# Rows of every second expert built on TensorE instead of gathered, and each expert's down product moved behind the next expert's gate and up

## The chip, the cores and the metric

One core of one Trainium2 chip runs the whole program. The metric is the device time of one execution in microseconds (us), of which less is better.

## What is computed

Two transformer layers over 512 prompt tokens and 32 sample tokens (8 streams of 4), model width 1024, all in fp32. Layer 0 mixes with a latent attention (a cache of 4096 rows for each sample stream), layer 1 with a window attention. After each of them stands a mixture of 32 experts, and that is the part that the change touches:

```python
def hier_moe(x, w_group, b_group, w_expert, b_expert, w_gate, w_up, w_down):
    ...
    g_p, g_idx = lax.top_k(g_prob, 1)
    e_top, e_idx = lax.top_k(e_sel, TOP_K_IN_GROUP)          # 2 experts for a token
    gate = g_p * jax.nn.softmax(e_top, axis=-1)
    ...
    def run_block(args):
        xb, e = args
        hid = jax.nn.silu(xb @ w_gate[e]) * (xb @ w_up[e])   # 1024 -> 512
        return hid @ w_down[e]                               # 512 -> 1024
```

544 tokens with two experts each make 1088 rows over 32 experts, 34 on average. The weights of one expert are three matrices of 2 MiB, 6.29 MB together, and every expert's weights are read from HBM once a layer: 201 MB a layer.

## The kernel before

The kernel is written engine by engine, with semaphores between the engines; no scheduler moves anything, so the order of the lines is the order on each engine. `x`, the residual rows, lies in SBUF as five tiles of 128 tokens (`TILES` = 5). The expert part is `experts(L)`, which exists once for each engine. A block takes at most `BLK` = 64 rows of one expert; more rows would go through a second loop (`more_...`).

- **Which rows.** VectorE (DVE) makes a matrix of marks for expert q, `mark(q)`: 128 x 5 x 64, a one where a token of this tile is the expert's row r. TensorE (PE) multiplies the marks with token numbers (`numbers(q)`: 5 small matmuls), and DVE turns the product into an index list.
- **Fetching rows.** Normalized rows have been stored to HBM (`moe_rows_in`). GpSimd (POOL) gathers the rows of expert q by an indirect DMA into `xe[q % 2]`, `LOOK` = 3 experts ahead, and PE turns them by 8 transposes (`fetched_T`); ScalarE (ACT) copies them to `xeT` (`rows_T`). Only expert 0's rows are made otherwise: its marks, multiplied with each token's reciprocal root (`direct`), are PE's stationary operand, the raw rows `x` its moving one (10 matmuls of 512 columns), and DVE applies the gain while it copies the turned rows to `xeT[0]`.
- **The expert.** PE: gate and up for k = 0..7 (16 matmuls of 64 x 512 outputs), then the transposes of the next expert's rows, `numbers(e + 3)`, 4 transposes of `hid`, and down (8 matmuls). ACT computes the silu, DVE the product `hid`, and the copy `hidT` of the turned `hid`. ACT and DVE copy half each of the result out (`y0_ready`, `y1_ready`), and POOL scatters it to HBM (`moe_rows_back`).
- **Weights.** SyncE (SP) issues the loads in the order gate, up, down of expert 3, 4, and so on, into `SLOTS` = 3 buffers. Its wait rule, which the change leaves alone, is:

```python
def follow(e, s):
    sp.wait_ge(sig["gu_mm"], happened("gu_mm", NE * L + e - 2))   # gate and up of expert e - 3 done
    gate_up(e, s)
    sp.wait_ge(sig["d_mm"], happened("d_mm", NE * L + e - 2))     # down of expert e - 3 done
    down(e, s)
```

Each fp32 matmul stands as two MATMUL records in the trace: the 24 of an expert's down and the next one's gate and up are "x48". PE's matmuls are recorded at L1941 and its transposes at L1946, both helpers; L996 is the silu, L1600 the product `hid`, L1605 the copy `hidT`, L1611 the copy of the result, L681 the gather, L691 the scatter, L500 the gate and up loads, L505 the down loads.

Of the kernel before, what the change touches and what calls it, by code (L numbers as in the profile page):

```python
# [8 lines left out]
ALU = mybir.AluOpType  # L9
# [39 lines left out]
INTO = ((FETCHES + 1) // 2 - 1, FETCHES // 2)  # L49
# [128 lines left out]
def build(nc, a, o):  # L178
    with ExitStack() as ctx:
# [168 lines left out]
        jrep = r.take(P)  # L348
        router = Arena(mem, oT_end, moe_end - 96 - P)
# [252 lines left out]
        def _(g):  # L602
# [42 lines left out]
            def experts(L):  # L645
# [22 lines left out]
                for b in range(2):  # L668
                    g.memset(xe[b], 0.0)
# [25 lines left out]
                for q in range(1, LOOK):  # L695
                    fetch(q, q % 2)
                with g.Fori(0, NE // 2) as i:
                    for b in range(2):
                        fetch(2 * i + b + LOOK, 1 - b)
                        store(2 * i + b, b)  # L700
                for b in range(2):
                    g.wait_ge(sig[f"gathered{b}"], landed(f"gathered{b}", INTO[b] * (L + 1)))
                    g.wait_ge(sig[f"scattered{b}"], landed(f"scattered{b}", STORES * (L + 1)))
# [44 lines left out]
        def _(act):  # L748
# [211 lines left out]
            def experts(L):  # L960
# [28 lines left out]
                act.wait_ge(sig["first_mm"], happened("first_mm", L + 1))  # L989
                copy(sg[0:BLK, :], ps[0:BLK, 5, :]).then_inc(sig["first_act"], 1)  # L990
                with act.Fori(0, NE // 2) as i:
                    for b in range(2):
                        e = 2 * i + b
                        act.wait_ge(sig["gu_mm"], happened("gu_mm", NE * L + e + 1))
                        act.wait_ge(sig["hid_ready"], happened("hid_ready", NE * L + e))
                        act.activation(sg[BLK:2 * BLK, :], ps[0:BLK, b, :], ACT.Silu).then_inc(sig["silu_ready"], 1)  # L996
                        rows_T(e + 1, 1 - b)
                        act.wait_ge(sig["d_mm"], happened("d_mm", NE * L + e + 1))
                        act.wait_ge(sig[f"scattered{b}"], landed(f"scattered{b}", STORES * L + i + 1))
                        copy(ye[b][0:BLK, 0:FF], ps[0:BLK, 2 + b, :]).then_inc(sig["y0_ready"], 1)  # L1000
# [124 lines left out]
        def _(v):  # L1125
# [358 lines left out]
            def experts(L):  # L1484
# [62 lines left out]
                for q in range(LOOK):  # L1547
# [3 lines left out]
                    if q == 0:  # L1551
                        v.drain()
                        v.tensor_tensor(direct, onehot[0], rstd[:, 0:TILES].unsqueeze(2).broadcast_to([P, TILES, BLK]), ALU.mult
                                        ).then_inc(sig["direct_ready"], 1)
                    else:
                        numbers(q - 1, (q - 1) % 2)

                v.wait_ge(sig["first_mm"], happened("first_mm", L + 1))
# [14 lines left out]
                v.tensor_copy(lt[0:NE, 2:3], ps[0:NE, 4, 8:9])  # L1573
# [9 lines left out]
                v.drain().then_inc(sig["list_ready"], 1)  # L1583
                v.wait_ge(sig["listrow_mm"], happened("listrow_mm", L + 1))
                v.tensor_copy(lst[0:1, 0:LIST], ps[0:1, 4, 16:16 + LIST])
                v.tensor_copy(lst[0:1, 2 * NE - 1:2 * NE], ps[0:1, 4, 40:41])
                v.tensor_tensor(jstart, ps[:, 4, 64:64 + LIST], idx[:, 0:LIST], ALU.add)
# [3 lines left out]

                numbers(LOOK - 1, (LOOK - 1) % 2)
                with v.Fori(0, NE // 2) as i:
                    for b in range(2):
                        e = 2 * i + b
                        v.wait_ge(sig["idx_mm"], happened("idx_mm", FETCHES * L + e + LOOK - 1))
                        mark(e + LOOK, 1 - b)
                        v.wait_ge(sig["silu_ready"], happened("silu_ready", NE * L + e + 1))
                        v.wait_ge(sig["ht_mm"], happened("ht_mm", NE * L + e))
                        v.tensor_tensor(hid[0:BLK, :], sg[BLK:2 * BLK, :], ps[BLK:2 * BLK, b, :], ALU.mult  # L1600
                                        ).then_inc(sig["hid_ready"], 1)
                        numbers(e + LOOK, 1 - b)
                        v.wait_ge(sig["ht_mm"], happened("ht_mm", NE * L + e + 1))
                        v.wait_ge(sig["d_mm"], happened("d_mm", NE * L + e))
                        v.tensor_copy(hidT, ps[:, 6, 0:KF * BLK].rearrange("p (k t) -> p k t", k=KF)  # L1605
                                      ).then_inc(sig["hidT_ready"], 1)
                        v.wait_ge(sig[f"scattered{b}"], landed(f"scattered{b}", STORES * L + i + 1))
                        v.tensor_copy(store_at[b][0:BLK, :], store_rows[0:BLK, cols(e, 1)])
                        v.drain()
                        v.wait_ge(sig["d_mm"], happened("d_mm", NE * L + e + 1))  # L1610
                        v.tensor_copy(ye[b][0:BLK, FF:D], ps[BLK:2 * BLK, 2 + b, :]).then_inc(sig["y1_ready"], 1)  # L1611
                for b in range(2):
                    v.wait_ge(sig[f"scattered{b}"], landed(f"scattered{b}", STORES * (L + 1)))
                    v.wait_ge(sig[f"gathered{b}"], landed(f"gathered{b}", INTO[b] * (L + 1)))
# [322 lines left out]
        def _(pe):  # L1937
# [341 lines left out]
            def experts(L):  # L2279
# [24 lines left out]
                def fetched_T(q, b, fetched):  # L2304
# [414 lines left out]
```

## Time and profile before

| | |
|---|---|
| median of 3 runs | 1850.82 us (1849.52 to 1857.86) |
| the profiled execution, its own time | 1853.15 us |
| its span in the trace | 1851.5 us |
| TensorE busy | 1668.3 us, 90% |
| VectorE, ScalarE, GpSimd busy | 29%, 23%, 13% |
| HBM read | 507 MB, of which 403 MB are expert weights |

The two expert parts run from about 504 to 1019 us and from about 1304 to 1819 us. Times inside the trace count from the span's start.

### The profile page before, as it was taken

What the parts mean: (1) busy time and instruction counts of PE and PEld (TensorE: products, weight loads), DVE (VectorE), ACT (ScalarE), POOL (GpSimd) and SP (SyncE); (2) the same over time, 40 slices, a digit from 0 to 9 for tenths busy, and PEclk for the clock granted to TensorE, in tenths of its full rate; (3) what the DMA queues carried; (4) which work ended last, traced back from release to release, by engine and by line L of the source; (5) the groups of instructions that cost most, each with busy time, mean ns of one, the idle gap of its engine ahead of it and who ended that gap; (6) DMA issues with size and microseconds to landing.
All of it is one profiled execution on the core that took longest, in us unless ns stands there. A gap on an engine that the chain in (4) does not pass through costs nothing.

```text
span 1851.5 us, 27694 instructions
## 1 busy us (share of the span) xinstructions
PE 1668.3 (90%) x9306; PEld 876.0 (47%) x9307; DVE 542.5 (29%) x1490; ACT 420.5 (23%) x888; POOL 248.1 (13%) x348
## 2 busy tenths in 40 slices
PE   7899899999888989898989899999898989898885
PEld 5466666655544444444334445455444444444332
DVE  2334343332421111111111556754211111111113
ACT  2233344421111111111111224342011111111112
POOL 1131014400011111111111200000111111111110
PEclk9899899999988999999989999999799999998997
DMA  5253137764469999999998800032999999999984
GB/s 180 65 155 89 50 119 250 258 256 198 166 231 409 407 411 409 403 411 409 409 411 355 300 20 1 20 137 83 360 400 415 414 412 408 410 402 405 404 347 151
DMA packets 83342, 515.60 MB, mean 278 GB/s; under 512 B 22664, under 2 KB 41049, under 8 KB 56794
## 3 DMA queue, kind: packets, MB, share of 16 engines
q1 hardware_dynamic: 61962, 461.35, 62.5%
q0 software_dynamic: 21296, 53.15, 8.8%
q8 instruction: 50, 0.82, 0.2%
q14 instruction: 34, 0.28, 0.1%
HBM read 506.99 MB, written 26.52 MB: 288 GB/s over the span
## 4 chain that ended last, share of the span: by engine, by line
PE 76%; DMA 7%; issue 6%; DVE 6%; ACT 3%; DVEq 1%; ACTq 0%; SPq 0%; POOLq 0%
PE ps L1941 66%; PE ps L1946 10%; DMA mem<-in_moe_w_up 4%; DMA mem<-moe_rows_back 1%; DVE mem L1600 1%; ACT mem L996 1%; ACT mem L752 1%; DVE mem L1719 0%; DMA mem<-in_mla_w_a 0%; DMA moe_rows_back<-mem 0%; DVE mem L1645 0%; DVE mem L1310 0%; ACT mem L923 0%; ACT mem L926 0%; DVE mem L1758 0%
## 5 line engine op out<-in xcount | busy, mean ns | idle before, releaser
L1941 PE MATMUL ps<-mem 128*64 128x512 f32 (+13 forms) x7330 | 1430.0, 493 | 101.6 <-issue 49.5
L1941 PEld LDWEIGHTS ps<-mem 128*64 128x64 f32 (+4 forms) x7330 | 646.8, 150 | 794.1 <-issue 707.5
L752 ACT ACTIVATE mem<-ps 128x512 f32<-128x512 f32 (+3 forms) x370 | 205.8, 568 | 720.5 <-PE ps L1941 523.1
L1946 PE MATMUL ps<-mem 128*128 128x128 f32 (+1 forms) x1976 | 273.7, 280 | 74.1 <-DVE mem L1600 45.7
L1946 PEld LDWEIGHTS ps<-mem 128*128 128x128 f32 (+1 forms) x1976 | 234.3, 171 | 172.8 <-issue 151.2
L1600 DVE TENSOR_TENSOR mem<-mem,ps 64x512 f32<-64x512 f32 x64 | 44.2, 690 | 469.6 <-ACT mem L996 469.6
L681 POOL DMA_INDIRECT mem<-moe_rows_in,mem x68 | 63.4, 933 | 557.0 <-issue 539.9
L1611 DVE COPY mem<-ps 64x512 f32<-64x512 f32 x64 | 44.4, 694 | 310.0 <-PE ps L1941 310.0
L691 POOL DMA_INDIRECT moe_rows_back<-mem x64 | 59.2, 925 | 352.7 <-DVE mem L1611 346.2
L996 ACT ACT_TABLE_LOAD x32 | 41.1, 1283 | 231.8 <-PE ps L1941 231.8
L996 ACT ACTIVATE mem<-ps 64x512 f32<-64x512 f32 x64 | 37.7, 589 | 198.6 <-PE ps L1941 198.2
L1298 DVE COPY mem<-ps 128x512 f32<-128x512 f32 x64 | 44.2, 692 | 76.2 <-PE ps L1946 72.1
L642 POOL DMA_DIRECT2D mem<-in_cache_mla x96 | 51.7, 538 | 103.7 <-PE ps L1941 93.7
L622 POOL DMA_DIRECT2D mem<-in_cache_mla x64 | 34.6, 540 | 114.5 <-issue 114.5
L1036 ACT ACTIVATE mem<-mem 128x256 f32<-128x256 f32 (+1 forms) x64 | 30.3, 474 | 61.6 <-DVEq L1724 61.6
L663 POOL DMA_DIRECT2D moe_rows_in<-mem x10 | 5.4, 538 | 237.7 <-DVE mem L1426 237.7
L1605 DVE COPY mem<-ps 128x256 f32<-128x256 f32 x64 | 27.2, 425 | 24.5 <-PE ps L1946 20.6
L1719 DVE CUSTOM_DVE_ANT_0 mem<-ps,mem 128x256 f32<-128x256 f32 (+1 forms) x64 | 26.3, 448 | 27.2 <-PE ps L1941 25.1
L1535 DVE TENSOR_TENSOR mem<-mem 128x320 f32<-128x320 f32 x70 | 33.7, 482 | 1.5 <-issue 0.7
L867 ACT ACTIVATE mem<-mem 128x128 f32<-128x128 f32 (+3 forms) x32 | 18.0, 562 | 37.8 <-DVEq L1247 37.8
L1645 DVE SCALAR_TENSOR_TENSOR mem<-mem 128x1024 f32<-128x1024 f32 (+1 forms) x16 | 20.5, 1281 | 20.5 <-DMA mem<-moe_rows_back 19.7
L769 ACT ACTIVATE mem<-mem 128x1024 f32<-128x1024 f32 x10 | 10.6, 1057 | 65.7 <-DVEq L1391 53.6
(233 smaller groups left out, 461.1 us busy)
## 6 DMA issues: line engine op xcount, KB each, us to landing
mem<-in_moe_w_gate SPq DMA_DIRECT2D x64, 2048.0 KB, 17.5
mem<-in_moe_w_up SPq DMA_DIRECT2D x64, 2048.0 KB, 24.8
mem<-in_moe_w_down SPq DMA_DIRECT2D x64, 2048.0 KB, 22.0
mem<-in_cache_mla POOLq DMA_DIRECT2D x160, 160.0 KB, 4.4
mem<-in_cache_mla SPq DMA_DIRECT2D x96, 160.0 KB, 5.4
mem<-moe_rows_back SPq DMA_DIRECT2D x8, 1024.0 KB, 8.5
mem<-in_mla_wo SPq DMA_DIRECT2D x1, 4096.0 KB, 14.3
moe_rows_in<-mem POOLq DMA_DIRECT2D x8, 512.0 KB, 3.0
```

The source lines that it names most:

```text
L622: g.dma_start(pages_flat[par][:, bass.ds(j * ROW, ROW)], a["cache_mla"][0][bass.ds(page, 1)].rearrange("a p c -> p (a c)")).then_inc(sig[f ...
L642: g.dma_start(pages[b % 2][:, j, :], a["cache_mla"][0][bass.ds(at[n], 1)].rearrange("a p c -> p (a c)")).then_inc(sig[f"late_pages{b % 2}" ...
L681: g.indirect_dma_start(out=xe[b][0:BLK, :], out_offset=None, in_=rows_in, in_offset=bass.IndirectOffsetOnAxis(ap=fetch_at[b][0:BLK, 0:1].b ...
L691: g.indirect_dma_start(out=rows_back, out_offset=bass.IndirectOffsetOnAxis(ap=store_at[b][0:BLK, 0:1].bitcast(U32), axis=0), in_=ye[b][0:B ...
L752: return act.activation(out, in_, ACT.Copy)
L996: act.activation(sg[BLK:2 * BLK, :], ps[0:BLK, b, :], ACT.Silu).then_inc(sig["silu_ready"], 1)
L1298: v.tensor_copy(kT[t % 2][:, n], ps[:, bank, :].rearrange("p (g c) -> p g c", g=2)).then_inc(sig[f"tp_ev{bank}"], 1)
L1535: v.tensor_tensor(onehot[b], rankm[:, :, cols(q, 1)].broadcast_to([P, TILES, BLK]), slots.unsqueeze(1).broadcast_to([P, TILES, BLK]), ALU. ...
L1600: v.tensor_tensor(hid[0:BLK, :], sg[BLK:2 * BLK, :], ps[BLK:2 * BLK, b, :], ALU.mult).then_inc(sig["hid_ready"], 1)
L1611: v.tensor_copy(ye[b][0:BLK, FF:D], ps[BLK:2 * BLK, 2 + b, :]).then_inc(sig["y1_ready"], 1)
L1941: return pe.matmul(out, lhsT, rhs, start=start, stop=stop)
L1946: return pe.transpose(out, in_, ident[at:at + n, at:at + n])
```

## The change

1. Expert 2, 4, 6 ... get their rows as expert 0 did: after its own gate and up, PE multiplies the marks (times the reciprocal root, now in an array `marks`) with the raw rows into PSUM bank 7 (`rows_made(k)`, 10 matmuls), ACT and DVE copy half each to `xe[0]` (`made(k)`), PE turns them, and DVE copies them to `xeT[0]` with the gain (`made_T`). The gathers into `xe[0]` are gone: 17 of 34 a layer, those of experts 2, 4 ... 30 and two empty ones. `rows_made` is done for k = 1 to 16 (k = 16 is an empty block), so 16 times 10 matmuls a layer are added.
2. PE's order in the loop is `gate_up(e + 1)`, then `rows_made` if e is odd, then `down(e)`, then the transposes, the numbers and the turned `hid` of e + 1 (`turns`). ACT's and DVE's loops follow it.
3. Before the loop, `gate_up(0)` comes right after expert 0's rows; the list of experts with more than 64 rows is made behind it, in PSUM bank 3 instead of 4.

```diff
@@ POOL
-                for q in range(1, LOOK):
-                    fetch(q, q % 2)
+                fetch(1, 1)
                 with g.Fori(0, NE // 2) as i:
-                    for b in range(2):
-                        fetch(2 * i + b + LOOK, 1 - b)
-                        store(2 * i + b, b)
+                    fetch(2 * i + LOOK, 1)
+                    store(2 * i, 0)
+                    store(2 * i + 1, 1)
@@ ACT
+                def made(k):
+
+                    act.wait_ge(sig["first_mm"], happened("first_mm", MADE * L + k + 1))
+                    copy(xe[0][0:BLK, 0:FF], ps[0:BLK, 7, :]).then_inc(sig["first_act"], 1)
+
+                def follow(i, b):
+
+                    e = 2 * i + b
+                    silu(e + 1, 1 - b)
+                    if b:
+                        made(i + 2)
+                    rows_back_0(e, i, b)
+                    if b:
+                        rows_T(e + 2, 1)
@@ DVE
+                def made_T(q):
+
+                    v.wait_ge(sig["xt_mm"], happened("xt_mm", (NE + 1) * L + q + 1))
+                    v.tensor_tensor(xeT[0], ps[:, 5, :].rearrange("p (k t) -> p k t", k=KD),
+                                    gainT_ffn[:, L].unsqueeze(2).broadcast_to([P, KD, BLK]), ALU.mult).then_inc(sig["xeT_ready"], 1)
+
+                def hidden(e, b, i=None):
+
+                    v.wait_ge(sig["idx_mm"], happened("idx_mm", FETCHES * L + e + LOOK - 1))
+                    mark(e + LOOK, 1 - b)
+                    if i is not None:
+                        v.drain()
+                        v.wait_ge(sig["first_mm"], happened("first_mm", MADE * L + i + 2))
+                        v.tensor_tensor(marks, onehot[0], rstd[:, 0:TILES].unsqueeze(2).broadcast_to([P, TILES, BLK]), ALU.mult
+                                        ).then_inc(sig["direct_ready"], 1)
...
+                def follow(i, b):
+
+                    e = 2 * i + b
+                    if b:
+                        hidden(e + 1, 0)
+                        made(i + 2)
+                    else:
+                        hidden(e + 1, 1, i)
+                    rows_back_1(e, i, b)
+                    if b == 0:
+                        made_T(e + 2)
+                    hidden_T(e + 1, 1 - b)
@@ PE
+                def rows_made(k):
+
+                    pe.wait_ge(sig["direct_ready"], happened("direct_ready", MADE * L + k + 1))
+                    pe.wait_ge(sig["first_act"], happened("first_act", MADE * L + k))
+                    turnstile(pe)
+                    pe.wait_ge(sig["first_dve"], happened("first_dve", MADE * L + k))
+                    for T in range(TILES):
+                        for c in range(2):
+                            last = mm(ps[c * BLK:(c + 1) * BLK, 7, :], marks[:, T, :], xt(T, P, c * FF, (c + 1) * FF),
+                                      T == 0, T == TILES - 1)
+                    last.then_inc(sig["first_mm"], 1)
...
+                def follow(i, r):
+
+                    gate_up(i, r + 1)
+                    if r % 2:
+                        rows_made(3 * i + (r + 1) // 2 + 1)
+                    down(i, r)
+                    turns(i, r + 1)
```

What PE does between expert 0's turned rows and the loop. Before, in the order of the program (x8 are expert 0's transposes, 32x1 to 128x18 the list of overfull experts, 64x2 the numbers of expert 2; the gate and up of expert 0 are the first rows of the loop):

```order
L1946 MATMUL ps<-mem 128x64 x8
L1941 MATMUL ps<-mem 32x1
L1941 MATMUL ps<-mem 1x18
L1941 MATMUL ps<-mem 1x1
L1941 MATMUL ps<-mem 128x18
L1941 MATMUL ps<-mem 64x2 x5
L2374 UNCONDITIONAL_BRANCH
```

The same place of the changed kernel (the 26 are expert 0's gate and up and the 10 matmuls of expert 2's rows; the last x8 and x4 turn expert 1's rows and expert 0's `hid`):

```order
L2021 MATMUL ps<-mem 128x64 x8
L2016 MATMUL ps<-mem 64x512 x26
L2016 MATMUL ps<-mem 32x1
L2016 MATMUL ps<-mem 64x2 x5
L2021 MATMUL ps<-mem 128x64 x8
L2016 MATMUL ps<-mem 1x18
L2016 MATMUL ps<-mem 1x1
L2016 MATMUL ps<-mem 128x18
L2016 MATMUL ps<-mem 64x2 x5
L2021 MATMUL ps<-mem 128x64 x4
L2492 UNCONDITIONAL_BRANCH
```

The gate and up of expert 0 stand ahead of the list now, and before expert 0's down comes the whole gate and up of expert 1.

Inside PE's loop, from the turned `hid` of one expert on. Before (x4 turns `hid`, x8 is the same expert's down, x16 the next one's gate and up, the last x8 the rows of the one after it):

```order
L1946 MATMUL ps<-mem 128x64 x4
L2362 ISA
L1941 MATMUL ps<-mem 64x512 x8
L2342 REGISTER_ALU
L1941 MATMUL ps<-mem 64x512 x16
L1946 MATMUL ps<-mem 128x64 x8
```

The changed kernel, at an expert in front of which rows are made (x16 is the next expert's gate and up, x18 the 10 matmuls of made rows and the 8 of down):

```order
L2021 MATMUL ps<-mem 128x64 x4
L2428 REGISTER_ALU
L2016 MATMUL ps<-mem 64x512 x16
L2381 REGISTER_ALU
L2016 MATMUL ps<-mem 64x512 x18
L2393 ISA
L2021 MATMUL ps<-mem 128x64 x8
```

Behind the turned `hid` PE no longer goes to down, which needs the copy `hidT`, but to a gate and up that doesn't.

ACT's loop. Before (L996 the silu, 128x512 the copy `xeT`, 64x512 the result):

```order
L996 ACT_TABLE_LOAD
L996 ACTIVATE mem<-ps 64x512
L986 REGISTER_ALU
L752 ACTIVATE mem<-ps 128x512
L999 ISA
L752 ACTIVATE mem<-ps 64x512
L996 ACTIVATE mem<-ps 64x512
```

In the changed kernel (L995 the silu):

```order
L995 ACT_TABLE_LOAD
L995 ACTIVATE mem<-ps 64x512
L752 ACTIVATE mem<-ps 64x512
L752 ACTIVATE mem<-ps 128x512
L1021 UNCONDITIONAL_BRANCH
L1021 ISA
L994 REGISTER_ALU
L995 ACTIVATE mem<-ps 64x512
```

The table load stood inside the loop, once for every two experts; it stands ahead of the loop now, once for a layer.

## Rows read from the trace of the kernel before

**Rows 1.** The page: its first line, busy time by engine, GB/s in 40 slices.

```profile
span 1851.5 us, 27694 instructions
...
PE 1668.3 (90%) x9306; PEld 876.0 (47%) x9307; DVE 542.5 (29%) x1490; ACT 420.5 (23%) x888; POOL 248.1 (13%) x348
...
GB/s 180 65 155 89 50 119 250 258 256 198 166 231 409 407 411 409 403 411 409 409 411 355 300 20 1 20 137 83 360 400 415 414 412 408 410 402 405 404 347 151
```

**Rows 2.** Critical chain, layer 0, experts 3 to 5: start us, us, what.

```profile
561.84 12.77 PE ps L1941 x48
574.61 1.03 PE ps L1946 x8
575.63 0.67 PE ps L1941 x10
576.31 0.62 PE ps L1946 x4
576.93 0.71 issue
577.64 10.53 PE ps L1941 x48
588.35 1.21 issue
...
592.72 12.22 PE ps L1941 x48
```

**Rows 3.** Load of expert 5's up weights: issue (ns, start us), us to landing.

```profile
L500 SPq DMA_DIRECT2D mem<-in_moe_w_up x1: 383/383/383, 557.9 to 557.9; - x1
...
DMA to landing us min/median/max: 17.2/17.2/17.2
```

**Rows 4.** The same for expert 31.

```profile
L500 SPq DMA_DIRECT2D mem<-in_moe_w_up x1: 435/435/435, 963.9 to 963.9; - x1
...
DMA to landing us min/median/max: 37.7/37.7/37.7
```

**Rows 5.** The same, all 29 up loads of layer 0's loop.

```profile
DMA to landing us min/median/max: 13.0/28.6/41.8
```

**Rows 6.** Critical chain, the last experts of layer 0.

```profile
913.73 40.88 DMA mem<-in_moe_w_up
...
1014.05 5.10 PE ps L1941 x16
```

**Rows 7.** Windows, layers 0, 1: busy (records) PE PEld DVE ACT POOL, PEclk, DMA share, GB/s.

```profile
553.00:940.00 387.00, 350.08 (x1755) 158.54 (x1752) 66.32 (x175) 61.13 (x88) 46.39 (x51) 0.92 1.01 408
1366.00:1750.00 384.00, 348.91 (x1750) 160.76 (x1748) 67.46 (x175) 59.85 (x87) 46.33 (x50) 0.92 1.01 409
```

**Rows 8.** The same, short windows in layer 0 and before it.

```profile
446.00:455.00 9.00, 9.00 (x24) 3.98 (x23) 0.00 (x0) 0.00 (x0) 0.00 (x0) 1.00 1.00 430
...
703.40:708.60 5.20, 5.20 (x28) 1.87 (x26) 1.09 (x2) 0.59 (x1) 0.93 (x1) 1.00 1.02 378
...
735.20:740.20 5.00, 5.00 (x26) 2.07 (x24) 1.09 (x2) 0.59 (x1) 0.93 (x1) 1.00 0.98 347
709.80:713.60 3.80, 3.80 (x30) 2.10 (x26) 0.00 (x0) 1.46 (x2) 0.00 (x0) 1.00 1.01 426
```

**Rows 9.** Timeline: a gather and a scatter: start us, us, engine, what.

```profile
700.37 0.93 POOL L681 DMA_INDIRECT mem<-moe_rows_in,mem  x1 [7.48 <-issue]
...
706.81 0.93 POOL L691 DMA_INDIRECT moe_rows_back<-mem  x1 [5.51 <-DVE mem L1611]
```

**Rows 10.** Timeline, start of layer 0's experts: start us, us, engine, what.

```profile
513.12 0.76 DVE L1568 TENSOR_TENSOR mem<-ps,mem 128x256 f32<-128x256 f32 x2 [0.42 <-PE ps L1946]
...
516.74 10.22 PE L1941 MATMUL ps<-mem 128*64 128x2 f32 x42 [0.78 <-DVEq L1590]
...
536.92 0.35 SPq L505 DMA_DIRECT2D mem<-in_moe_w_down  x1
...
543.92 0.34 SPq L500 DMA_DIRECT2D mem<-in_moe_w_gate  x1
```

More of the change, by code:

```diff
@@ L48 @@
 FETCHES = NE + LOOK
[L49 removed]
+INTO = (0, FETCHES // 2)
+MADE = NE // 2 + 1
 SAVES = ((TILES + 1) // 2, TILES // 2)
@@ L987, in rows_T, with silu @@
                     copy(xeT[b], ps[:, 5, :].rearrange("p (k t) -> p k t", k=KD)).then_inc(sig["xeT_ready"], 1)
-                act.wait_ge(sig["first_mm"], happened("first_mm", L + 1))
+                act.wait_ge(sig["first_mm"], happened("first_mm", MADE * L + 1))
                 copy(sg[0:BLK, :], ps[0:BLK, 5, :]).then_inc(sig["first_act"], 1)
[L991 to L1000, printed above, removed]
+                def silu(e, b):
+                    act.wait_ge(sig["gu_mm"], happened("gu_mm", NE * L + e + 1))
+                    act.wait_ge(sig["hid_ready"], happened("hid_ready", NE * L + e))
+                    act.activation(sg[BLK:2 * BLK, :], ps[0:BLK, b, :], ACT.Silu).then_inc(sig["silu_ready"], 1)
@@ new lines, in follow @@
+                def follow(i, b):
[6 more added lines that the diff above has]
+                        rows_T(e + 2, 1)
+                silu(0, 0)
+                made(1)
+                rows_T(1, 1)
+                with act.Fori(0, NE // 2 - 1) as i:
+                    follow(i, 0)
+                    follow(i, 1)
+                rows_back_0(NE - 2, NE // 2 - 1, 0)
@@ L1001, in experts @@
+                silu(NE - 1, 1)
+                rows_back_0(NE - 1, NE // 2 - 1, 1)
                 act.wait_ge(sig["lst_ready"], happened("lst_ready", L + 1))
@@ new lines, in follow @@
+                def follow(i, b):
[9 more added lines that the diff above has]
+                    hidden_T(e + 1, 1 - b)
+                numbers(LOOK - 1, (LOOK - 1) % 2)
+                hidden(0, 0)
+                made(1)
@@ L1590, in experts @@
                 v.drain().then_inc(sig["lst_ready"], 1)
[L1592 to L1611, printed above, removed]
+                hidden_T(0, 0)
+                with v.Fori(0, NE // 2 - 1) as i:
+                    follow(i, 0)
+                    follow(i, 1)
+                rows_back_1(NE - 2, NE // 2 - 1, 0)
+                hidden(NE - 1, 1)
+                made_T(NE)
+                hidden_T(NE - 1, 1)
+                rows_back_1(NE - 1, NE // 2 - 1, 1)
                 for b in range(2):
                     v.wait_ge(sig[f"scattered{b}"], landed(f"scattered{b}", STORES * (L + 1)))
-                    v.wait_ge(sig[f"gathered{b}"], landed(f"gathered{b}", INTO[b] * (L + 1)))
+                    v.wait_ge(sig["gathered1"], landed("gathered1", INTO[1] * (L + 1)))
                 n = v.value_load(lst[0:1, 2 * NE - 1:2 * NE], min_val=0, max_val=LIST)
@@ L2351, in expert, with hidden_T @@
                     last.then_inc(sig["gu_mm"], 1)
-                    fetched_T(e + 1, 1 - b, (odd if b == 0 else even) + pair + 1)
-                    numbers(e + LOOK, 1 - b)
+                def hidden_T(e):
                     pe.wait_ge(sig["hid_ready"], happened("hid_ready", NE * L + e + 1))
@@ L2361, in expert, with turns, down @@
                     last.then_inc(sig["ht_mm"], 1)
+                def turns(i, r):
+                    e, b, _, _ = place(i, r)
+                    fetched_T(e + 1, 1 - b, 3 * i + (r + 1) // 2)
+                    numbers(e + LOOK, 1 - b)
+                    hidden_T(e)
+                def down(i, r):
+                    e, b, s, turn = place(i, r)
                     pe.wait_ge(sig[f"d{s}_in"], landed(f"d{s}_in", turn))
```

99 lines of the change are left out of this document (69 added, 30 removed).

## The prediction

> **What bounds the kernel now.** The page first: TensorE is busy 90% of 1851.5 us, and in the slices of both expert parts the DMA engines move some 410 GB/s [rows 1]. So two things may be the bound, and each stage has to say which. In the middle of the experts the chain of waits runs through PE alone: from one x48 (an expert's down and the next one's gate and up) at 561.84 to the next but one at 592.72 are 30.88 us, 15.4 an expert, with no weight load in it [rows 2]. That would make it PE's. But the time from issue to landing of the up weights grows: 17.2 us for expert 5, 37.7 for expert 31 [rows 3, 4], 41.8 at the most [rows 5], and near the end the chain does go through such a load, 40.88 us of it [rows 6]. Expert 5's up weights land at 557.9 + 17.2 = 575.1, expert 31's at 963.9 + 37.7 = 1001.6: 26 experts in 426.5 us, 16.4 an expert. **So the DMA engines are the slower side all the time (16.4 against PE's 15.4), and PE only lives on the head start of three buffers, which is used up at the end.** The window rows agree: the DMA share is 1.01 over nearly the whole of both parts, at 408 and 409 GB/s, PE's clock 0.92 [rows 7]. What is worth anything is therefore what makes the stream of weights end earlier, and what stands behind it.
>
> **What a gather costs the stream.** Undisturbed, the engines move 430 GB/s [rows 8]: 6.29 MB take 14.6 us, so 1.8 us an expert go elsewhere. A gather is issued at 700.37 [rows 9], its rows flow 3 us later. In 703.4 to 708.6 the rate is 378 GB/s: 1966 KB against 2236 at 430. About 139 KB of the 1966 are the gathered rows (34 rows of 4 KB), so the weights lose 409 KB, 0.95 us. The window of another, 735.2 to 740.2, at 347 GB/s: 2150 - (1735 - 139) = 554 KB, 1.29 us. Mean 1.1 us. The scatter issued at 706.81 shows 426 GB/s in its window: 1634 - (1619 - 139) = 154 KB, 0.36 us [rows 8, 9]. A gather thus costs three times its bytes, a scatter about its bytes; both together 1.5 of the 1.8 us.
>
> Here the Trainium skill would say otherwise. In DMA: Bandwidth & Descriptors, section Queues, rings and completion order, each DMA engine takes turns between the queues it has work for, packet by packet; by that alone a gather would cost its bytes, 0.33 us, as the scatter does, and the sum below would lose two thirds of its gain (rival 1). The gather windows of [rows 8] speak for the dearer figure at the gathers.
>
> **The change, part by part.**
>
> *PE, added.* `rows_made` is 10 matmuls. 24 matmuls take 10.53 us at the full clock [rows 2], 0.44 each: 4.4 us for every second expert, 2.2 an expert. *PE, removed.* Before, PE waits 1.21 us and longer for the silu (with a table load in every second expert) and 0.71 us for the copy `hidT` before every down; the 12.77 against 10.53 us of two x48 is the clock, which falls to half for a while behind such a stop [rows 2]. In the new order the silu and `hid` of e + 1 have down(e) (3.5 us), 8 transposes (1.03) and the numbers (0.67) as cover, and `hidT` has a gate and up (7.0). The tightest cover is that of `made_T`: DVE first copies the result, then turns to the 128x512 product, which takes 0.76 (the same size in [rows 10]); with as much for the copy of half that size the product is done some 1.9 us after down; PE gets to the next gate and up 1.03 + 0.67 + 0.62 = 2.3 us after it. It fits by 0.4 us; if it didn't, the shortfall would count once for two experts. PE's new pace: two experts are 2 x (10.5 + 1.03 + 0.67 + 0.62) + 4.4 = 30.0 us, 15.0 an expert, hardly less than the 15.4 of now: the made rows take back nearly all that the order gives. A gathered row set (odd experts) is issued two experts ahead as before, so nothing waits for it; DVE and ACT have room (29% and 23% busy, [rows 1]).
>
> *DMA, removed.* 17 gathers a layer, 15 of them with rows. Those of experts 2 and 4 flow while the stream still has gaps. I count the 13 of experts 6 to 30 between the landings of expert 5 and expert 31: 13 x 1.1 = **14.3 us a layer**. The stream's pace becomes 16.4 - 0.55 = 15.85 us, still slower than PE's 15.0. So the DMA engines keep being the bound, and the next thing that is late is again a gate and up weight: PE's head start (about 14 us at expert 5, below) is gone after some 17 experts.
>
> *Start of a layer, moved.* SP issues down(3) and gate_up(4) behind expert 0's down, and this now comes behind the whole gate and up of expert 1. Now: down(3) at 536.92, gate_up(4) at 543.92 [rows 10]. After: `xeT[0]` is ready at 513.9, gate and up of expert 0 (9 us, partly at half clock) ends at 522.9, made rows 4.4, numbers, 8 transposes, list, numbers, `hid` turned 4.0, gate and up 7.0, down 3.5: 541.8. That is down(3) 4.9 us later, gate_up(4) 2.1 earlier. Gate and up of 3 are issued 4.2 us earlier, land, and then the engines stand idle for some 7 us. Second step: transposes 2.3, gate and up 7.0, made rows 4.4, down 3.5: at 559.0 the loads of down(4) and gate_up(5) are issued. The first bytes of a load come about 3 us after its issue (the least time to a landing is 13.0 for an up load, which stands behind a gate load: two times 4.9 and 3, [rows 5]). Three matrices of 2.1 MB at 430 GB/s are 14.6 us, so expert 5's up weights land at 577.2 with a scatter, where they land at 575.1 now [rows 3]: **2.1 us a layer lost**. From there on SP has always more than an expert's loads out, so the stream has no further gap.
>
> *End of a layer.* Expert 31's up weights land at 1001.6 [rows 4], PE ends at 1014.05 + 5.10 = 1019.15 [rows 6]: 17.5 us. The last expert's down, silu and copies stand as before; the table load is gone from the loop, one waiting start at half clock may come in. I take the tail as equal.
>
> *Sum.* Layer 0 ends at 1019.15 - 14.3 + 2.1 = 1007.0, 12.2 us earlier; what follows is unchanged. PE alone would allow more: from 541.8 the 31 remaining downs, 30 gate and ups, 31 rounds of transposes and numbers, 15 made rows are 108.5 + 210 + 72 + 66 = 456.5 us and about 4 for the last expert, whose waits nothing covers: 1002.3. So the margin of PE below the DMA engines is only 5 us a layer. Both layers have the same pace [rows 7]: 24.4 us in all. 1853.15 (the profiled execution's own time, 2.3 above the median) - 24.4 = 1828.8, and 1826.5 on the scale of the median 1850.8. I say **1827**.
>
> **Rivals.** A measurement of this kernel tells 0.5% (9 us) from no change, not less.
>
> 1. *A removed gather gives back only its bytes.* For it: the scatter's 0.36 us [rows 8]; the loss at a gather might come from something that the other gathers and the weights then fill anyway. Then 13 x 0.35 = 4.6 us - 2.1 = 2.5 a layer: 1850.8 - 5 = 1846, no change that can be told. Against it: the two gather windows. This is also where the rule on taking turns leads. Chance 0.13.
> 2. *PE becomes the bound.* If one of the covers fails by 1 us or so for every pair, or the clock falls often, PE's pace goes from 15.0 to 15.6, and the layer ends at 541.8 + 460.5 + 31 x 0.6 = 1020.9: nothing is won, 1850 to 1854. Above 15.54 us an expert it decides for no gain, above 16 (a stop of 2 us for each pair, as the silu's is now) for **slower**: 1019.15 becomes about 1033, so 1850.8 + 2 x 14 = 1879. For it: PE waits for weights near the end and would do so at half clock (1.7 us more each, 12.22 against 10.53 in [rows 2]); 10 matmuls for each pair are a sure cost. Against it: stops at half clock come only when PE waits for the stream, and then it is the stream that counts. Chance of no change by this 0.05, of slower by over 0.5% 0.07.
> 3. *More is won.* The slowest DMA engine decides when a load has landed, and a gather of 34 rows may load some of the 16 more than others: 16.4 - 14.6 - 0.36 would give up to 1.4 us a gather; with a start that loses nothing and a tail that wins 1 us, 19 us a layer: 1813. Chance 0.15.
>
> **How the numbers follow.** The forecast's own case (PE fits, gather at 0.95 to 1.3 us, start 1 to 4 us) has 0.60 and spans 1820 to 1836; with rival 3 that is 0.75 for faster. Rival 1 and the mild half of 2 give 0.18 for the same, the rest 0.07 slower. The range for 8 in 10 takes in rival 3 and the cheap side of the gather's price up to half of rival 1: 1812 to 1844.
>
> **What would show it.** Right: no rows of a gather for even experts; PE's chain without the 1.21 and 0.71 us stops in the first half of a layer, clock near 1.0 there, x48 and x20 at 0.44 us a matmul; later waits of a gate and up for its weights already from expert 20 or so; landings of up weights 15.9 us apart instead of 16.4; a gap in the DMA share at the start of layer 0's experts before 545 us. Wrong: weights landing 16.2 us apart or more (rival 1); PE's x20 behind a wait for ACT or DVE in the middle of a layer, and a time to landing that doesn't grow (rival 2).

## The result, and the profile after

The changed kernel takes 1844.66 us (median of 15 runs, 1841.29 to 1852.07); the kernel before, run beside it, 1853.53 us. The ratio, worked out over all runs and so not quite that of the medians, is 0.9949, with a 95% interval of 0.9937 to 0.9961: 9 us, or half a per cent, are won. One of the 17 runs of the kernel before that stand beside experiments 1, 2, 3 and 6 took 3562 us and is left out of the ratios. The forecast was 1827 us, a gain of 24. The profiled execution has a span of 1842.6 us against 1851.5 [rows 1], 8.9 us less.

The page of the changed kernel: span, busy time by engine, GB/s in 40 slices, and two of its DMA queues (packets, MB, share of 16 engines; q1 carries the weights, q0 the gathers and scatters).

```profile
span 1842.6 us, 29042 instructions
...
PE 1743.9 (95%) x9946; PEld 871.1 (47%) x9947; DVE 602.8 (33%) x1586; ACT 381.9 (21%) x858; POOL 214.1 (12%) x312
...
GB/s 181 68 155 88 50 116 237 254 253 208 159 182 404 414 421 417 412 419 419 415 418 350 303 14 1 20 138 85 347 375 412 422 414 418 414 421 408 418 307 151
...
q1 hardware_dynamic: 61962, 461.35, 62.1%
q0 software_dynamic: 18576, 49.16, 8.1%
```

PE is busy 95% now, and the full slices of the expert parts stand at 404 to 422 GB/s where they stood at 400 to 415: both sides moved. PE's chain in the middle of a layer, for comparison with [rows 2] (start us, us, what; x68 is gate and up, 10 matmuls of made rows, and down; x48 the same without made rows):

```profile
547.02 14.74 PE ps L2016 x68
561.77 1.03 PE ps L2021 x8
562.79 0.67 PE ps L2016 x10
563.47 0.62 PE ps L2021 x4
564.09 10.45 PE ps L2016 x48
...
576.86 14.74 PE ps L2016 x68
```

From one x68 to the next are 29.84 us, 14.9 an expert, without a stop and at the full clock: the "issue" rows of 0.71 and 1.21 us are gone. So the order does on PE what it was forecast to do. The windows of the changed kernel (columns as in [rows 7]) say the same of the stream:

```profile
533.00:537.00 4.00, 4.00 (x14) 1.27 (x12) 1.47 (x5) 0.00 (x0) 1.25 (x1) 0.57 0.70 285
537.00:541.00 4.00, 4.00 (x20) 1.34 (x18) 0.00 (x0) 0.00 (x0) 0.00 (x0) 1.00 0.02 6
541.00:545.00 4.00, 4.00 (x21) 1.41 (x18) 1.09 (x3) 0.76 (x2) 0.00 (x0) 1.00 0.00 0
561.00:565.00 4.00, 4.00 (x32) 2.58 (x30) 1.78 (x5) 1.19 (x2) 0.92 (x1) 1.00 0.67 209
553.00:940.00 387.00, 382.38 (x2022) 158.62 (x2020) 91.22 (x214) 45.57 (x77) 34.88 (x38) 0.98 1.00 415
1366.00:1750.00 384.00, 376.37 (x1986) 156.47 (x1984) 90.00 (x211) 43.79 (x74) 33.79 (x37) 0.98 1.01 416
```

The last two rows answer to [rows 7]: the clock is 0.98 instead of 0.92. The others show what is lost: PE's granted clock is 0.57 for 4 us; for 8 us, 537 to 545, the DMA engines move next to nothing (6 and 0 GB/s); and from 561 to 565 they move half of what they could. The loads of expert 5's and expert 31's up weights, as in [rows 3, 4]:

```profile
L502 SPq DMA_DIRECT2D mem<-in_moe_w_up x1: 381/381/381, 562.8 to 562.8; - x1
...
DMA to landing us min/median/max: 19.0/19.0/19.0
...
L502 SPq DMA_DIRECT2D mem<-in_moe_w_up x1: 432/432/432, 963.5 to 963.5; - x1
...
DMA to landing us min/median/max: 29.3/29.3/29.3
```

They land at 581.9 and 992.7: 410.8 us for 26 experts, 15.8 each, where it was 426.4. The same reading for both kernels and both layers, in us (up(5) is the landing of expert 5's up weights; "end" is the end of the last expert's down, "tail" the time from up(31) to it):

| | layer 0: up(5), up(31), between | end, tail | layer 1: up(5), up(31), between | end, tail |
|---|---|---|---|---|
| before | 575.1, 1001.5, 426.4 | 1019.2, 17.6 | 1376.7, 1802.5, 425.9 | 1817.7, 15.1 |
| after | 581.9, 992.7, 410.9 | 1012.9, 20.2 | 1373.9, 1786.8, 412.9 | 1808.4, 21.6 |

**Where the time went.** Layer 0: its experts begin 0.9 us later (DVE's product on expert 0's turned rows starts at 514.02 instead of 513.12, a difference of what stands ahead of it), up(5) lands another 5.8 us later, the interval is 15.5 us shorter, the tail 2.6 us longer: 1019.2 + 0.9 + 5.8 - 15.5 + 2.6 = 1013.0. Layer 1 begins 6.5 us earlier (the gate load of expert 1 is issued at 1282.74 instead of 1289.19; by DVE's product, as in layer 0, it would be 5.7, and the loss at up(5) 2.9); up(5) loses 3.7 of it, the interval wins 13.0, the tail loses 6.5: 9.3 us in all, 2.8 of them its own. So the interval gave on average the 14.3 us that were forecast, and start and tail took back 8.4 us in layer 0 and 10.2 in layer 1.

The tail is seen in the chain. The changed kernel, end of layer 0 and end of layer 1:

```profile
943.60 34.23 DMA mem<-in_moe_w_up
...
977.87 14.81 PE ps L2016 x68
...
995.00 0.71 issue
995.72 10.52 PE ps L2016 x48
...
1706.25 34.06 DMA mem<-in_moe_w_up
...
1740.36 16.51 PE ps L2016 x68
...
1771.96 14.74 PE ps L2016 x68
...
1789.76 11.89 PE ps L2016 x48
...
1804.70 3.67 PE ps L2016 x16
```

The last x68 of each layer (977.87, 1771.96) holds the 10 matmuls of block k = 16, which is empty, between gate and up of expert 30 and the down of 29. In layer 1 the last wait for the stream ends at 1706.25 + 34.06 = 1740.31, 68 us before the end: from there on PE is the later side, and the half clock behind the wait (16.51 against 14.74) and behind the stop of 0.74 us for `hidT` (11.89 against 10.45) is paid in full.

The same x48, the down of 30 and the gate and up of 31, in the kernel before, layers 0 and 1:

```profile
998.79 12.22 PE ps L1941 x48
...
1798.83 12.09 PE ps L1941 x48
```

It begins 2.7 and 3.7 us ahead of the landing of up(31) there, and 3.0 us behind it in both layers of the changed kernel. So PE is later by 5.7 and 6.6 us against the stream. What differs between the layers is the clock: the kernel before pays 3.1 us to the lower level in layer 0's tail (12.22, and 5.10 in [rows 6], where the full clock takes 10.53 and 3.67) and 1.6 in layer 1's (12.09); the changed kernel pays nothing and 1.4 (11.89). That makes 5.7 - 3.1 = 2.6 and 6.6 - 1.6 + 1.4 = 6.4, against 2.6 and 6.5 measured.

### The profile page after: what moved, and what is told of

It is laid out like the page before. It is cut to its first block, busy times and chain, and to the rows that moved or that the text cites. A ratio compares the mean times of both kernels' runs of the same rounds, so it can differ in the third digit from the quotient of the medians.

```text
span 1842.6 us, 29042 instructions
## 1 busy us (share of the span) xinstructions
PE 1743.9 (95%) x9946; PEld 871.1 (47%) x9947; DVE 602.8 (33%) x1586; ACT 381.9 (21%) x858; POOL 214.1 (12%) x312
## 4 chain that ended last, share of the span: by engine, by line
PE 75%; DMA 14%; DVE 5%; issue 2%; ACT 2%; DVEq 1%; SPq 0%; POOL 0%; ACTq 0%; POOLq 0%
PE ps L2016 65%; DMA mem<-in_moe_w_up 11%; PE ps L2021 10%; ACT mem L752 1%; DMA mem<-in_x_sample 1%; DMA mem<-in_c_masks 1%; DVE mem L1794 0%; DMA mem<-moe_rows_back 0%; DMA mem<-in_cache_mla 0%; DMA moe_rows_back<-mem 0%; DVE mem L1765 0%; DMA mem<-in_swa_sinks 0%; DVE mem L1336 0%; ACT mem L923 0%; ACT mem L926 0%
## 5 line engine op out<-in xcount | busy, mean ns | idle before, releaser
L2016 PE MATMUL ps<-mem 128*64 128x512 f32 (+14 forms) x7970 | 1510.1, 485 | 62.2 <-DMA mem<-moe_rows_back 14.0
L752 ACT ACTIVATE mem<-ps 128x512 f32<-128x512 f32 (+4 forms) x370 | 205.7, 567 | 621.9 <-PE ps L2016 425.2
L995 ACT ACTIVATE mem<-ps 64x512 f32<-64x512 f32 x64 | 37.7, 589 | 557.8 <-PE ps L2016 557.8
L1653 DVE COPY mem<-ps 64x512 f32<-64x512 f32 x64 | 44.4, 693 | 147.2 <-PE ps L2016 147.2
L1617 DVE COPY mem<-ps 64x512 f32<-64x512 f32 x32 | 22.2, 694 | 89.4 <-PE ps L2016 89.4
L682 POOL DMA_INDIRECT mem<-moe_rows_in,mem x34 | 33.2, 977 | 79.3 <-issue 79.3
L1622 DVE TENSOR_TENSOR mem<-ps,mem 128x512 f32<-128x512 f32 x32 | 22.1, 692 | 9.8 <-PE ps L2021 9.7
```

What stands on the lines that cost most here:

```text
L682: g.indirect_dma_start(out=xe[b][0:BLK, :], out_offset=None, in_=rows_in, in_offset=bass.IndirectOffsetOnAxis(ap=fetch_at[b][0:BLK, 0:1].b ...
L752: return act.activation(out, in_, ACT.Copy)
L2016: return pe.matmul(out, lhsT, rhs, start=start, stop=stop)
```

## The experiments

Theory A, from the readings above: a gather costs the stream some 1.2 us, the change takes 13 a layer away; at the start the SyncE queue holds back gate_up(4) and (5) behind the later downs, and at the end the added matmuls stand on the path. Rivals are named with each run. Experiments 1, 2, 3 and 6 ran on one chip with 17 runs of the kernel before (median 1855.28 us), experiments 4, 5, 7 and 8 on another with 9 (1855.6 us). Each has one trace, so a difference of a few tenths of a microsecond between two traces is not read.

**1. before_half_gathers.** The kernel before, without the gathers of the even experts; nothing takes their place.

```diff
-                        fetch(2 * i + b + LOOK, 1 - b)
+                        if b == 0:
+                            fetch(2 * i + b + LOOK, 1 - b)
...
```

> The kernel before, with the gathers of experts 2, 4, 6 ... left out and nothing in their place: these experts work on rows of zeros, so their part of the result is left out. PE's order and work are those of before. Theory A (a gather costs the stream of weights 1.0 to 1.2 us, and PE with its 15.4 us an expert stands close behind the stream): between the landings of expert 5's and expert 31's up weights are 411 to 414 us instead of 426, but the time falls by 5 to 10 us only (1844 to 1849), because PE alone needs 31 x 15.44 us from expert 0's down at 536.9, that is 1015.5 against 1019.15. Theory B (a removed gather gives back its bytes, 0.35 us): the landings are 421 to 423 us apart and the time falls by 0 to 6 us.

Measured: 1844.04 us, 0.9936 (0.9916 to 0.9956). Up(5) lands at 573.8, up(31) at 983.0: 409.2 us between (layer 1: 410.3), where it was 426.4, a little shorter than theory A said (411 to 414); the time is in its range. Theory B (421 to 423) is refuted. The load of expert 31's up weights in this kernel:

```profile
L500 SPq DMA_DIRECT2D mem<-in_moe_w_up x1: 434/434/434, 955.9 to 955.9; - x1
...
DMA to landing us min/median/max: 27.1/27.1/27.1
```

So 13 gathers cost 17.2 us of stream, 1.3 each (15.6 and 1.2 in layer 1). And yet the time falls by no more than in the changed kernel: the stops of the old order are still there, PE needs its 15.4 us an expert, and the stream is no longer what it waits for. With the gathers gone and nothing else, PE is the bound: from 900 us to the end of the layer its chain holds no weight load, and the layer ends at 1010.5, 27.5 us behind the landing of up(31). The gain of the change (0.9949) is not larger than that of the gathers alone.

**2. order_with_gathers.** The changed kernel with all gathers back and no made rows: the order alone.

```diff
-INTO = (0, FETCHES // 2)
-MADE = NE // 2 + 1
+INTO = ((FETCHES + 1) // 2 - 1, FETCHES // 2)
+MADE = 1
...
-                    if r % 2:
-                        rows_made(3 * i + (r + 1) // 2 + 1)
```

> The changed kernel's order on all engines (down behind the next gate and up), but the rows of every expert gathered, none made but expert 0's. Theory A: the stream of weights is the bound at 16.4 us an expert as before, PE needs only 12.8; the later first down costs the stream some 3 us a layer and the deferred down 2 to 4 us at the layer's end, so the time is 6 to 14 us above before (1.003 to 1.008). Rival (PE's stops were what bounded the kernel, and the made rows took the gain back): the time falls, by up to 20 us.

Measured: 1857.24 us, 1.0006 (0.9991 to 1.002); the span is 1856.6, 5.1 above that of the profile before. Landings 580.2 and 1006.0 in layer 0, 425.8 us between, as before. Up(5) of layer 0 is 5.1 us later, but 1.6 of that was there before the experts began (DVE's product on expert 0's rows ends at 515.1 instead of 513.5), so the order costs some 3.5 there, against 3 expected. In layer 1 the product is 5.0 us later and up(5) only 3.3 (1380.0 against 1376.7): no loss. The order shortens nothing while the stream is the bound. The time is 1 to 2 us above before and not told from none, below the range that I had put down (6 to 14); the one trace's span is 5 us longer. The rival, that the time falls, is refuted. The tail is 17.6 us in layer 0 and 17.0 in layer 1; the changed kernel's is longer by 2.6 and 4.6, which belongs to the made rows. But the order isn't free there either: the last x48 begins 0.4 us behind up(31) and 0.3 ahead of it (1006.39, 1805.39), so 3.1 and 3.4 later against the stream than in the kernel before. At 10.52 us it runs at the full clock in both layers, where the kernel before had 12.22 and 12.09, and that hides it.

**3. made_old_order.** The changed kernel with down(e) ahead of gate and up of e + 1 on PE.

```diff
-                    gate_up(i, r + 1)
-                    if r % 2:
-                        rows_made(3 * i + (r + 1) // 2 + 1)
                     down(i, r)
+                    gate_up(i, r + 1)
+                    if r % 2:
+                        rows_made(3 * i + (r + 1) // 2 + 1)
```

> The changed kernel with one swap on PE: down(e) stands in front of gate_up(e + 1) again; rows made and the order of ACT and DVE stay. Theory A: PE's pace is 15.6 to 15.8 us an expert (2 x (10.5 + 2.3 + 0.7 for hidT) + 4.4, no table load), the stream needs 15.9, so both bind; the first down comes 8 us earlier and the stream starts without a gap. The time is 0 to 12 us above before. Rival (the new order is worth all of the gain and made rows cost their full 4.4 us for each pair): 50 us or more above before.

Measured: 1955.47 us, 1.0536 (1.0511 to 1.0561). My figure missed widely and the rival's held. Its chain, one pair of experts:

```profile
604.47 0.71 issue
605.19 10.52 PE ps L2016 x48
...
618.19 1.61 issue
619.80 16.51 PE ps L2016 x68
```

PE stops for `hidT` 0.71 and 1.61 us before the downs, and behind the longer stop the x68 runs partly at half clock (16.51 against 14.81). Up weights now land 17.2 us apart (579.7 to 1025.9), 15.4 us after their issue at expert 5 and 14.5 at expert 31: the time to landing no longer grows, so the loads wait for PE.

**4. made_old_order_fitted.** But ScalarE and VectorE still stood in the order of the changed kernel there. This run fits them: both copy the result of e ahead of silu and `hid` of e + 1.

```diff
 ACT
+                    rows_back_0(e, i, b)
                     silu(e + 1, 1 - b)
                     if b:
                         made(i + 2)
-                    rows_back_0(e, i, b)
 DVE
+                    rows_back_1(e, i, b)
                     if b:
                         hidden(e + 1, 0)
...
-                    rows_back_1(e, i, b)
```

> made_old_order again (made rows, but down(e) ahead of gate and up of e + 1 as in the kernel before), with ScalarE and VectorE fitted to it: both copy the result of expert e ahead of silu and hid of e + 1. Theory A (the old order itself cannot carry the added matmuls: the kernel before has 15.4 us an expert with its stops, and 2.2 more are added): 17.0 to 17.6 us an expert in the middle of a layer, 1.04 to 1.06 of the kernel before. Rival (made_old_order was slow only because its copies stood in the wrong order): 16.0 to 16.5 us an expert, 1.00 to 1.02.

Measured: 1903.14 us, 1.0266 (1.0243 to 1.0289). Neither theory's ratio: it lies between. The pace is the rival's (below, 16.4 us), the ratio nearer to theory A's. Its chain:

```profile
581.96 0.71 issue
582.67 14.81 PE ps L2015 x68
...
599.80 0.71 issue
600.52 10.52 PE ps L2015 x48
...
613.36 0.71 issue
614.08 14.81 PE ps L2015 x68
```

The undisturbed pair takes 31.4 us, 15.7 an expert; the landings, 575.2 to 1002.3, give 16.4 on average, since now and then an x48 or x68 behind such a stop runs partly at half clock (567.28 12.22 for an x48). From 553 to 940 us PE is idle 17.2 of 387 us, which is 0.71 for each of 24 experts, and the granted clock is 0.96: 4% of 16.4 us are the missing 0.7. So of the 100 us that made_old_order loses, half was the order of the copies, and half the old order on PE itself: its 0.71 us for `hidT` stands before every down, and with the made rows PE is, on average, slower than the stream and has no head start left. Landings 16.4 us apart are also what the kernel before has, but there the stream sets them and PE runs ahead at 15.4; here PE sets them from the start (the loads land 14.6 us after issue at expert 5, 16.5 at expert 31), and layer 0 ends at 1044.5 instead of 1019.2.

**5. before_empty_gathers.** Is the price of a gather in its rows, or in its issue?

```diff
-                    v.tensor_scalar(fetch_at[b][0:BLK, :], ps[0:BLK, 4, 2 * b:2 * b + 1], FAR, None, ALU.add
+                    v.tensor_scalar(fetch_at[b][0:BLK, :], ps[0:BLK, 4, 2 * b:2 * b + 1], FAR if b else 3 * FAR, None, ALU.add
```

> The kernel before, but the gathers for experts 2, 4, 6 ... are issued with all indices out of bounds, so that they move no row (the result leaves out these rows' true content). All instructions stay. Theory (what a gather costs the stream is in moving the rows, three times their bytes): like before_half_gathers, expert 5's to expert 31's up weights 408 to 413 us apart instead of 426.4, 1839 to 1847 us, 0.992 to 0.996. Rival (the cost is in the issue: the list of descriptors is made and worked through whether or not a row moves): 423 to 427 us apart, 0.998 to 1.001.

Measured: 1845.0 us, 0.9942 (0.9922 to 0.9962), 410.8 us between up(5) and up(31) in layer 0, 411.0 in layer 1. As the theory said, time and interval: 15.6 of the 17.2 us are in the rows. Its queue q0 on the page, and that of before_half_gathers:

```profile
q0 software_dynamic: 21296, 49.15, 8.2%
```

```profile
q0 software_dynamic: 18576, 49.14, 8.1%
```

The packets of the issue are all there (21296), and cost nearly nothing (8.2% against 8.1%). The packet records of 580 to 960 us tell more, worked out over the records:

```
                       row packets   mean ns   weight packets   mean ns
before                 1707          180       9024             642
before_half_gathers    1268          174       9379             627
before_empty_gathers   1240          174       9361             628
order_with_gathers     1568          181       9071             641
after                  1263          175       9358             629
```

439 rows fewer are 13 gathers. Their own packets took 86 us over 16 engines, 0.4 us a gather. But each of the 9,400 weight packets also gets 15 ns shorter: 9379 x 15 / 16 = 8.8 us, 0.7 a gather. Together 1.1 of the 1.3 us. And they are slower just where a gather's rows flow. Over the same records, the weight packets that start 3 to 8.2 us after the issue of a gather (the place of the gather windows in [rows 8]) take 707 ns on average in the kernel before, the others 613 to 615. In before_empty_gathers it is 709 ns behind the gathers that move rows and 616 behind those that move none. So a gather slows the weight packets that flow beside it, and that costs more than its own rows take.

**6. short_last.** The changed kernel with 2 instead of 10 matmuls for the empty last block.

```diff
-                        rows_made(3 * i + (r + 1) // 2 + 1)
+                        rows_made(3 * i + (r + 1) // 2 + 1, 1 if isinstance(i, int) and r == 5 else TILES)
...
```

> The changed kernel, with the last made rows of a layer (an empty block) made with 2 matmuls instead of 10. Theory A (behind the last gate and up weights PE is the bound, and this block and the deferred down stand in its way): 3 to 3.6 us a layer less than the changed kernel, 6 to 8 us in all, ratio to before 0.991. Rival (the stream of weights is the bound to the end): no difference to the changed kernel, 0.995.

Measured: 1839.04 us, 0.9903 (0.9884 to 0.9921). The last x68 is an x52 of 11.38 us, and the tails are 16.8 and 19.6 us, 3.4 and 2.0 less than in the changed kernel; the medians differ by 5.6 us, the ratios by 0.46% (8.5 us), where 6 to 8 were expected. The empty block stood on the path. In layer 1 the x52 is 3.4 us shorter too (11.31 against 14.74), but the x68 behind the last wait took 17.76 us instead of 16.51, more of it at the lower clock.

**7. sp_order.** SyncE issues gate_up(e + 1) ahead of down(e), the order in which PE now uses them.

```diff
-                def follow(e, s):
+                def next_gate_up(e, s):
 
                     sp.wait_ge(sig["gu_mm"], happened("gu_mm", NE * L + e - 2))
                     gate_up(e, s)
+
+                def follow(e, s, after):
+
+                    next_gate_up(e + 1, after)
                     sp.wait_ge(sig["d_mm"], happened("d_mm", NE * L + e - 2))
                     down(e, s)
...
```

> The changed kernel with one edit: SyncE issues gate and up of expert e + 1 ahead of down of expert e, which is the order in which TensorE now uses them. Theory (the start of a layer is lost because the queue waits for down(0) before gate_up(4), and so on): gate_up(4) is issued some 8 us earlier than in the changed kernel (545.3 there), gate_up(5) some 7 us earlier (561.8), up(5) lands 5 to 8 us earlier in both layers, up(31) 10 to 12 us earlier (it also no longer stands behind down(30), 4.9 us). TensorE alone can end layer 0 at about 1002, the changed kernel ends it at 1012.9, so at most 10.8 us a layer can come back: 7 to 10 us a layer, 1825 to 1831 us, 0.985 to 0.989 of the kernel before. Rival (the gap at the start is not the queue's order, or the later down weights now stop TensorE): landings as in the changed kernel, or waits for down weights in the chain; 1840 to 1848 us, 0.993 to 0.998.

Measured: 1829.67 us, 0.986 (0.984 to 0.988). Time and ratio are in the range. Gate_up(4) is issued at 540.0 instead of 545.3 (5.3 us earlier, 8 expected), gate_up(5) at 552.8 instead of 562.4 (9.6, 7 expected). The windows of the kernel sp_order:

```profile
541.00:545.00 4.00, 4.00 (x31) 2.26 (x28) 1.87 (x4) 0.59 (x1) 0.00 (x0) 1.00 1.01 356
561.00:565.00 4.00, 4.00 (x30) 2.34 (x30) 1.77 (x6) 0.60 (x1) 1.88 (x2) 1.00 1.02 434
553.00:940.00 387.00, 387.00 (x2072) 161.93 (x2069) 94.56 (x221) 45.74 (x78) 35.68 (x39) 1.00 1.01 416
```

The second half of the first gap and the whole of the second are filled (0 and 209 GB/s in the changed kernel), and PE never stops in 387 us. Up(31) lands at 981.5, 11.2 us earlier, and layer 0 ends at 1004.4, 8.5 earlier than in the changed kernel, close to the 1002.3 at which PE alone can end. The landing of up(5) itself can't be read in full in this trace (4 records of its slot's landings are missing; those that there are end at 569.1, where it was 581.9); up(6) lands at 584.9 instead of 596.5. The gain at that place, 11.6 us, contains 4.9 us that are only the exchange of down(5) and gate_up(6) in the queue; 6.7 are the gaps. The half of the rival that feared the later down weights comes true once, at the end of layer 1, where PE stands idle 3.24 us for the down weights of expert 30, and the x48 behind them is partly at the lower clock:

```profile
1735.44 36.51 DMA mem<-in_moe_w_down
...
1772.23 13.15 PE ps L2022 x48
```

**8. sp_order_short_end.** The edits of sp_order and short_last together, and at the end of a layer gate and up of 31 ahead of down(30), with ScalarE and VectorE to match.

```diff
...
-                down(NE // 6, 0)
                 gate_up(NE // 6, 1)
+                down(NE // 6, 0)
                 turns(NE // 6, 1)
...
```

> The changed kernel with SyncE's order of sp_order, the empty last block of made rows cut from 10 matmuls to 2 as in short_last, and at the end of a layer gate and up of expert 31 ahead of down of expert 30 on TensorE, with ScalarE and VectorE to match. Theory: the stream is ahead by what sp_order wins and the tail by 3.5 us (8 matmuls) and some 3 us of down(30), which then covers the silu of 31: layer 0 ends near 996 instead of 1012.9, 12 to 17 us a layer, 1811 to 1821 us, 0.978 to 0.984 of the kernel before. Rival (the tail is set by the last down weights of the stream, not by what TensorE does in front of them): no more than sp_order alone wins, 0.985 to 0.989.

Measured: 1819.68 us, 0.9807 (0.9789 to 0.9825), which beats both kernels, the one before by 36 us. The end of its layer 0 in the chain:

```profile
930.53 35.84 DMA mem<-in_moe_w_up
...
966.41 12.70 PE ps L2022 x52
...
981.43 10.45 PE ps L2022 x48
...
994.21 0.71 issue
994.92 3.67 PE ps L2022 x16
```

The stop before the x48 of the last gate and up is gone (981.43 follows on PE's own work), and the layer ends at 998.6, 14.3 us before the changed kernel's 1012.9. It was put at 996; time and ratio are in the range.

## Why the prediction was half right

Right, by its own steps:

- **What bounds the kernel.** The stream, with PE close behind. Before_half_gathers shortens the stream by 17.2 and 15.6 us and wins only 11 us in all, because PE at 15.4 an expert then binds; order_with_gathers lets PE run freely and wins nothing.
- **Gathers, -14.3 us a layer.** Measured 15.5 and 13.0, mean 14.3; landings 15.8 and 15.9 us apart, forecast 15.85. The price of 1.1 us, read from windows of 5 us, is a little low (1.15 to 1.3 in experiments 1 and 5). That the mean meets the forecast to the tenth is luck: the layers are 2.5 us apart, and without its gathers the kernel before gains 17.2 and 15.6 us in the same interval, which the changed kernel does not reach; why, no run tells. Rival 1, that only the bytes come back, is refuted; it was also where the rule led that each DMA engine takes turns packet by packet (the Trainium skill, DMA: Bandwidth & Descriptors, Queues, rings and completion order). The rule may hold, but the weight packets get slower beside a gather's (709 against 616 ns in experiment 5), and that part it does not give.
- **PE's pace, 15.0.** Measured 14.9 in the first half of a layer, no stop, `made_T` fits. The first wait of the chain for weights in the middle of a layer is that for expert 20's, landing at 818.2 us, as forecast.

Wrong, and these make the difference between -24 and -9 us:

- **"Start of a layer, moved": 2.1 us a layer lost.** Measured 5.8 and 3.7. The first pass of the loop was put at PE's full clock, 10.5 us, and took 12.22, partly at the lower level of 1.2 GHz (granted clock 0.57 in 533 to 537; between 529 and 533 PE is busy 3.29 of 4 us): down(3) is issued at 544.7 instead of 541.8 and down(4) at 561.8 instead of 559.0, of which 0.9 was there before the experts began. Also, **"from there on ... the stream has no further gap"** stands on a start at 430 GB/s; in the 8 us after 565 it moved 411 and 394. The gap of 8 us ahead of 545 was seen in the forecast (7 us), but I took it as a price, and didn't see that the order of two loads in SyncE's queue set a part of it, and the gap after 561. Sp_order shows that.
- **"I take the tail as equal."** This is the step that failed most: 2.6 and 6.5 us. Two of the change's own parts were in my hands: block k = 16 with its 10 matmuls (4.3 us) comes after the last wait, with nothing behind which it could hide, and I counted it only in PE's average. And in the new order PE comes to the last x48 later against the stream even without made rows (3.1 and 3.4 us, experiment 2). With them it is 5.7 and 6.6 us later, and it is PE that ends the layer: in layer 0 it still has 35.1 us to go when up(30) lands at 977.8, and up(31) lands 14.9 us after that, which leaves the 20.2 us of tail. Short_last gives 3.4 and 2.0 us back. The lower clock I had priced at "one" start and then at nothing, because "stops at half clock come only when PE waits for the stream": but the chain of [rows 2] has no weight load and yet an x48 of 12.22 us behind a stop of 1.21, and the 11.89 of layer 1 stands behind one of 0.74 us for `hidT`. The kernel before pays for the clock in its tails too (3.1 and 1.6 us, the changed kernel 0 and 1.4), and that is why the tail grows by only 2.6 in layer 0 and by 6.5 in layer 1. What decides which start is slow, no run tells.
- **The sum's form.** PE alone was to end at 1002.3, the stream's side at 1007.0: a margin of 5 us was in the text, and with it the sum should have taken the later of two uncertain ends, not one of them. What goes wrong at such a margin can only make the time longer; the forecast's own case, 1820 to 1836, and the range up to 1844 left too little room on that side.

Together: start and tail were put at 4.2 us for both layers, and measured 8.4 + 10.2 = 18.6; the gathers gave 15.5 + 13.0 = 28.5. 28.5 - 18.6, less the 0.9 us lost ahead of layer 0's experts, is 9.0, and the span fell by 8.9.

Experiment 3 missed by more than the prediction did. There I took the made rows in the old order as hidden by the stream; PE had 15.4 and was given 2.2 more, against a stream of 15.8, which the same sum would have told.

## What to carry to other kernels

When two sides run within a few per cent of each other, a gain on one of them is worth its size only as long as the other allows it: work out both ends of each stage, and cost start and tail with the same care as the pace, because one-off costs count there in full. When the order in which an engine uses its operands changes, change the order in which they are loaded too; here that was worth more than the change itself (ratios to the kernel before: 0.986 against 0.9949). And look at what a loop computes in its last pass for nobody. One question stays open: leaving out half the gathers in the old order wins as much (0.9936) as the whole change, so on PE the new order does little more than pay for the made rows; whether these are still worth their matmuls with the new order of the loads, no run tells.

## What was not expected of the hardware

- An indirect gather of 34 rows of 4 KB costs the weight stream some 1.2 us, three to four times what its 139 KB take at 430 GB/s. Its own packets are 0.4 us of that; the weight packets beside it take 707 to 709 ns instead of 613 to 616, which lifts their average over a layer from 627 to 642 ns. What slows them is open: whether the source in HBM, the destination or the switching between queues does it, no run here separates. A gather whose indices are all out of bounds costs nearly nothing.
- A stop of PE of 0.71 us ahead of each down sometimes leaves the clock alone and sometimes makes the x48 behind it 12.22 instead of 10.52 us long, in the same kernel and loop (made_old_order_fitted: 567.28 against 600.52).
